# Two weight pieces of even attention split in quarters over four steps each

## The chip, the cores and the metric

The kernel runs on one core of one Trainium2 chip. The time is that of the device in microseconds (us), from the start to the end of one execution. Three executions of the kernel before were timed, and one more was recorded by the hardware profiler. The engines are TensorE (PE, whose weight loads are listed as PEld), VectorE (DVE), ScalarE (ACT), GpSimd (POOL) and SyncE (SP), whose queue issues the loads of weights.

## The reference

Three blocks run one after the other on 512 tokens of width 1024: a layer with even attention, a layer with differential attention, and a third block with neighbourhood attention and a gated recurrence. Each has an MLP of width 4096. The change lies in the first layer, in the attention that follows the input projection:

```python
def even_mixer(h, w_in, cmp_pe, cmp_w1, cmp_w2, w_out, cos, sin):
    ...
    qa = apply_rope(qa.reshape(bsz, T, A_HEADS, HEAD_DIM), cos, sin)
    ...
    o_a = dsa_attention(qa, ka, va, qi, ki, wi)
    ...
    o_b = nsa_attention(qb, k_c, v_c, k_s, v_s, k_w, v_w, gb, cmp_pe, cmp_w1, cmp_w2)
    o = jnp.concatenate([o_a.reshape(bsz, T, -1), o_b.reshape(bsz, T, -1)], axis=-1)
    return jnp.einsum('bte,ed->btd', o, w_out)
```

`dsa_attention` has 8 heads with one shared key and value; each query attends to the 128 keys that an index score picks (top-k). `nsa_attention` has 8 heads in two groups of keys and values and adds three gated branches: compressed, selected and window attention.

## The kernel before

**Weights in pieces and halves.** Products are made in three passes to keep float32 precision: a matrix is split into a high half, rounded to the type fp32r, and a low half, the rest. A product is high times high, high times low, and low times high. Weights come in pieces of 128 partitions by 2048 columns, loaded by SyncE into one of two buffers `stg`. ScalarE makes the high half `wh` (L381), VectorE the low half `wl` = `stg` - `wh` (L385). There are two buffers of each half. `split(e, key, ahead)` (L365) issues engine e's part for all pieces up to one behind `key` in the order in which TensorE takes them (`TAKES`). ScalarE's part waits for the load and for TensorE to have freed the halves of the piece two before; VectorE's waits for ScalarE's. SyncE refills a `stg` buffer when VectorE's part is done.

**The attention loop.** The work is cut into 52 units, each for a pair of heads and (but for the compressed ones) one block of 128 queries. Four groups of nine units come first (`cmp`, then `slc` and `win` for each of four query blocks), then 16 `dsa` units. Each engine runs a loop over steps n, one program per engine, in this order within a step:

- TensorE (`pe_even`): a part of "er" work if there is any, then the products with the values of unit n-4 (L1544, L1550), the transposes of unit n-3 (L1514), the scores of unit n (L1434, L1441, L1438; L1422 and L1425 for `cmp`).
- ScalarE (`act_even`): a rope copy (L1617) in some steps, the high half of a finished pair of heads (L1565) in some, the copy of the transposed weights of unit n-3 (L1530), the exponentials of unit n-1 (L1472), then `split_er`.
- VectorE (`dve_even`): the maximum of unit n-1 (L1461), the low half of a finished pair of heads (L1571) in some steps, the scaling of unit n-2 (L1496 and L1504; L1483 to L1492 for `cmp`), a rope addition (L1629, L1632) in some steps, then `split_er`, then one round of top-k (`take_more`, L1203 and L1205), as long as there are any, up to step 29.

**The "er" work** projects and rotates the queries of later heads in between, in parts of three: x = 0 and x = 1 are twelve matmuls each (L425), x = 2 the rotation (L1595). `ER_AT` puts a part into every third step. Piece `qa0` is taken in step 4, `qa2` in step 22, and the first piece of `out0`, the output projection, from step 50 on. `split_er` runs `split` in the step in which a piece is first taken, so piece `qa2` is split whole in step 4, and piece `("out0", 0, 0)` in step 22, on ScalarE and VectorE in the same step.

All waits are on semaphores, and each engine works through its queue in order. The loop's order is written out by hand.

Of the kernel before, what the change touches and what calls it, by code (L numbers as in the profile page):

```python
# [8 lines left out]
F32 = mybir.dt.float32  # L9
# [3 lines left out]
ALU = mybir.AluOpType  # L13
ACT = mybir.ActivationFunctionType
# [101 lines left out]
def build(nc, ins, out):  # L116
    ctx = ExitStack()
    with ctx:
# [5 lines left out]
        def signal(name, by=1):  # L124
            s = Signal(ctx.enter_context(nc.semaphore(name)), by)
            every.append(s)
            return s
# [86 lines left out]
        p_mm, p_turn, p_rot = signal("p_mm"), signal("p_turn"), signal("p_rot")  # L214
        p_score, p_flip, p_out, p_cmp, p_hg = [signal(n) for n in ("p_score", "p_flip", "p_out", "p_cmp", "p_hg")]
        a_hi, a_sq, a_part, a_keep, a_rope = [signal(n) for n in ("a_hi", "a_sq", "a_part", "a_keep", "a_rope")]
        a_up, a_exp, a_flip, a_misc, a_hg = [signal(n) for n in ("a_up", "a_exp", "a_flip", "a_misc", "a_hg")]
        v_lo, v_add, v_part, v_keep, v_rope = [signal(n) for n in ("v_lo", "v_add", "v_part", "v_keep", "v_rope")]
# [51 lines left out]
        for c in range(2):  # L270
            src = ins["even_w_out"][:, c * 512:(c + 1) * 512]
            piece(("out0", c, 1), 4, 512, [(whole, src[0:512, :].rearrange("(k p) n -> p k n", p=128))])
            hi = src[512:1024, :].rearrange("(g j d) n -> g d j n", g=2, j=4)
# [43 lines left out]
        ORDER, TAKES, SPLITS = [], [], []  # L317
# [4 lines left out]
        def stage_no(key):  # L322

            if is_block(key) and key[3:] == (1, 1):
                return 2
            return [k for k in ORDER if not (is_block(k) and k[3:] == (1, 1))].index(key) % 2

        def stage_of(key):
            kts, ncols, _, _ = SPEC[key]
            return (STG + [third])[stage_no(key)][:, 0:kts * ncols]  # L330

        def halves_of(key):
            kts, ncols, _, _ = SPEC[key]
            b = SPLITS.index(key) % 2
            return WH[b][:, 0:kts * ncols], WL[b][:, 0:kts * ncols]
# [18 lines left out]
        at_split = {}  # L354

        def whole_of(key):

            if key[3:4] != ("P",):
                return stage_of(key), piece_in[stage_no(key)].at(key)
            c = SEVEN[key[4]][1]  # L360
            if c in ("t1", "t2", "t3", "t4"):
                return (SB if c in ("t2", "t4") else SA), v_sum.at(key[0:3] + (c,))
            return stage_of(key[0:3] + c), piece_in[stage_no(key[0:3] + c)].at(key[0:3] + c)

        def split(e, key, ahead=1):  # L365

            last = TAKES.index(key) + ahead
            while at_split[e] <= min(last, len(TAKES) - 1):
                k = TAKES[at_split[e]]
                at_split[e] += 1  # L370
                if SPEC[k][3]:
                    continue
                n = SPLITS.index(k)
                hi, lo = halves_of(k)
                source, ready = whole_of(k)
                if e == "act":
                    act = engine[e]
                    act.wait_ge(*ready)
                    if n >= 2:
                        act.wait_ge(*p_mm.at(("free", SPLITS[n - 2])))  # L380
                    act.activation(hi, source, ACT.Copy).then_inc(*a_hi.next(k))  # L381
                else:
                    dve = engine[e]
                    dve.wait_ge(*a_hi.at(k))
                    dve.tensor_tensor(lo, source, hi.bitcast(F32), ALU.subtract).then_inc(*v_lo.next(k))  # L385

        engine = {}

# [139 lines left out]
        def act_add(act, tag, nk):  # L528
            for c in range(2):
                for g in range(nk // 4):  # L530
                    split("act", tag + (c, g))
                    yield

        def dve_add(dve, tag, nk, banks=range(8)):
            for c in range(2):
                for g in range(nk // 4):
                    split("dve", tag + (c, g))
                    for i in range(NT if g == nk // 4 - 1 else 0):
                        hc = h[:, i, c * 512:(c + 1) * 512]
                        dve.wait_ge(*p_mm.at((tag, c, i)))  # L540
                        dve.tensor_tensor(hc, hc, bank[banks[c * 4 + i]], ALU.add).then_inc(*v_add.next((tag, c, i)))
                    yield
# [56 lines left out]
        def act_add_norm(act, tag, norm, scratch=None):  # L599
# [13 lines left out]
            for g in range(2):  # L613
                split("act", tag + (0, g))
# [717 lines left out]
        def take_more(n):  # L1332
            for _ in range(n):
                next(taking["k"], None)
# [109 lines left out]
        def dve_max(dve, n):  # L1444
            m = small[n % 16]
            dve.wait_ge(*p_score.at(("even", n)))
            if UNITS[n][0] == "cmp":
                v = pair(n).rearrange("p g (a n) -> p g a n", n=32)
                dve.tensor_reduce(m[:, 0:8].rearrange("p (g a) -> p g a", g=2), v, AX.X, ALU.max).then_inc(
                    *v_max.next(("even", n, "max")))  # L1450
                dve.wait_ge(*v_max.now())
                dve.tensor_scalar(m[:, 0:8], m[:, 0:8], -1e28, None, ALU.max).then_inc(*v_max.next(("even", n, "low")))
                dve.wait_ge(*v_max.now())
                if n >= 4:
                    dve.wait_ge(*p_flip.at(("even", n - 4)))
                for g in range(2):
                    t = dve.tensor_tensor(PX[n % 4][:, g, 0:128].rearrange("p (a n) -> p a n", n=32), v[:, g],
                                          m[:, g * 4:g * 4 + 4].unsqueeze(2).to_broadcast([128, 4, 32]), ALU.subtract)
                t.then_inc(*v_max.next(("even", n)))
                return  # L1460
            dve.tensor_reduce(m[:, 0:2], pair(n), AX.X, ALU.max, negate=True).then_inc(*v_max.next(("even", n)))  # L1461
# [105 lines left out]
        def dve_head(dve, n):  # L1567
            if head_end(n):
                tag, j, (hi, lo) = head_end(n)
                dve.wait_ge(*a_part.at((tag, j)))  # L1570
                dve.tensor_tensor(lo, bank[6], hi.bitcast(F32), ALU.subtract).then_inc(*v_part.next((tag, j)))  # L1571

        ER = [(f"qb{j}", ("in", "qb2"), j - 2, qbT[:, j, :]) for j in (2, 3)]
        ER += [(f"qa{j}", ("in", f"qa{j // 2 * 2}"), j % 2, qaT[:, j, :]) for j in range(4)]
        ER_AT = {}
# [48 lines left out]
        def dve_er(dve, m):  # L1625
            name, _, _, dest = ER[m]
            dve.wait_ge(*p_rot.at(name))
            dve.wait_ge(*v_rope.at(ER[m - 2][0] if m >= 2 else f"qb{m}"))
            dve.tensor_tensor(TT[(2 * m + 1) % 4][:, 0:T], er_turned(m), sinT, ALU.mult).then_inc(*v_rope.next((name, "sin")))  # L1629
            dve.wait_ge(*g_cos.at(name))  # L1630
            dve.wait_ge(*v_rope.now())
            dve.tensor_tensor(dest, TT[2 * m % 4][:, 0:T], TT[(2 * m + 1) % 4][:, 0:T], ALU.add).then_inc(*v_rope.next(name))  # L1632

        def split_er(name, n):
            if n in ER_AT and ER_AT[n][1] == 0 and ER[ER_AT[n][0]][2] == 0:
                split(name, ER[ER_AT[n][0]][1])

        def pe_even(pe):

# [15 lines left out]
        def act_even(act):  # L1655
            for n in range(N_UNITS + 4):
                if n in ER_COPY:
                    act_er(act, ER_COPY[n])
                if n >= 4:
                    act_head(act, n - 4)  # L1660
                if 0 <= n - 3 < N_UNITS:
                    act_flip(act, n - 3)
                if 0 <= n - 1 < N_UNITS:
                    act_exp(act, n - 1)
                split_er("act", n)
                yield

        def dve_even(dve):
            for n in range(N_UNITS + 5):
                if 0 <= n - 1 < N_UNITS:  # L1670
                    dve_max(dve, n - 1)
                if n >= 5:
                    dve_head(dve, n - 5)
                if 0 <= n - 2 < N_UNITS:
                    dve_prob(dve, n - 2)
                if n in ER_AT and ER_AT[n][1] == 2:
                    dve_er(dve, ER_AT[n][0])
                split_er("dve", n)
                take_more(1)
                yield  # L1680

# [1701 lines left out]
```

## Time and profile before

| | us |
|---|---|
| median of 3 runs | 2228.25 |
| lowest and highest | 2227.51, 2230.23 |
| profiled execution, its own time | 2233.16 |
| span of the profiled execution | 2231.4 |
| TensorE busy in the span | 2131.4 |
| VectorE busy in the span | 1355.6 |
| ScalarE busy in the span | 920.9 |

### The profile page before, as it was taken

How to read it: one execution, taken by the hardware profiler on the slowest of the kernel's cores; microseconds unless marked ns; L12 is line 12 of the kernel's file. 1: busy time of each engine (PE TensorE's matmuls, PEld its weight loads, DVE VectorE, ACT ScalarE, POOL GpSimd, SP SyncE). 2: the span in 40 equal slices, each digit the busy share in tenths (PEclk: the TensorE clock that was granted, in tenths of full speed). 3: DMA queues.
4: the chain of work that ended last, by engine and by line, in shares of the span. 5: the costliest groups of instructions: out<-in, count | busy, mean ns of one | idle time of the engine just before them, and what ended most of it. 6: DMA issues, size and time to landing. Idle time of an engine off the chain costs nothing.

```text
span 2231.4 us, 27080 instructions
## 1 busy us (share of the span) xinstructions
PE 2131.4 (96%) x10767; PEld 1682.5 (75%) x10771; DVE 1355.6 (61%) x1995; ACT 920.9 (41%) x1485; POOL 223.3 (10%) x212
## 2 busy tenths in 40 slices
PE   6878888999999999999999999999999999999998
PEld 5765556888888776678888888766778768888887
DVE  4568853687773446756877745355656424678753
ACT  3214553545443334445454443143423223544542
POOL 2210000000000011100000003011145421000000
PEclk9989989999999999999999999999999999999999
DMA  5430101223332221113333323221112213342232
GB/s 143 116 95 20 20 1 57 95 95 113 105 100 98 79 76 57 38 57 104 95 114 111 97 95 108 79 63 47 57 50 65 72 42 114 104 132 82 97 105 76
DMA packets 163511, 182.64 MB, mean 82 GB/s; under 512 B 19701, under 2 KB 123562, under 8 KB 163386
## 3 DMA queue, kind: packets, MB, share of 16 engines
q1 hardware_dynamic: 161066, 174.11, 24.9%
q0 software_dynamic: 2320, 6.80, 1.2%
q8 instruction: 86, 1.41, 0.3%
q14 instruction: 39, 0.32, 0.0%
HBM read 177.75 MB, written 2.17 MB: 81 GB/s over the span
## 4 chain that ended last, share of the span: by engine, by line
PE 86%; DVE 8%; ACT 3%; issue 2%; DMA 1%; SPq 1%; POOL 0%; ACTq 0%; POOLq 0%; DVEq 0%
PE banks L425 70%; PE banks L2761 2%; DVE wl L385 2%; ACT wh L381 2%; PE banks L1514 1%; PE banks L1434 1%; PE banks L1550 1%; PE banks L2880 1%; DVE uTl L595 1%; PE banks L1958 1%; PE banks L2020 1%; PE banks L2451 1%; PE banks L2530 1%; PE banks L1882 1%; PE banks L2501 1%
## 5 line engine op out<-in xcount | busy, mean ns | idle before, releaser
L425 PE MATMUL banks<-uTh,wh 128*128 128x512 f32 (+1 forms) x1408 | 554.6, 394 | 14.1 <-DVE wl L385 4.2
L425 PE MATMUL banks<-uTl,wh 128*128 128x512 f32 (+1 forms) x1408 | 539.1, 383 | 0.0
L425 PE MATMUL banks<-uTh,wl 128*128 128x512 f32 (+1 forms) x1408 | 539.0, 383 | 0.0
L425 PE MATMUL banks<-wh,hTr 128*128 128x512 f32 x1552 | 487.4, 391 | 0.3 <-DVE hTr L2080 0.3
L385 DVE TENSOR_TENSOR wl<-stg,wh 128x2048 fp32r<-128x2048 f32 (+1 forms) x136 | 313.7, 2307 | 244.8 <-ACT wh L381 244.2
L381 ACT ACTIVATE wh<-stg 128x2048 fp32r<-128x2048 f32 (+1 forms) x136 | 258.6, 1902 | 209.2 <-PE banks L425 175.0
L425 PEld LDWEIGHTS banks<-wh,hTr 128*128 128x128 f32 x1552 | 291.6, 188 | 64.4 <-DVE wl L385 2.5
L425 PEld LDWEIGHTS banks<-uTh,wh 128*128 128x128 f32 x1408 | 268.6, 191 | 70.6 <-issue 10.3
L425 PEld LDWEIGHTS banks<-uTh,wl 128*128 128x128 f32 x1408 | 267.7, 190 | 52.4
L425 PEld LDWEIGHTS banks<-uTl,wh 128*128 128x128 f32 x1408 | 268.6, 191 | 50.2 <-issue 2.4
L425 PE MATMUL banks<-wl,hTr 128*128 128x512 f32 x776 | 302.5, 390 | 0.0
L425 PEld LDWEIGHTS banks<-wl,hTr 128*128 128x128 f32 x776 | 145.9, 188 | 29.2
L805 ACT ACTIVATE p<-banks 128x512 f32<-128x512 f32 x96 | 57.4, 597 | 209.1 <-PE banks L425 209.1
L502 POOL TENSOR_TENSOR nrm<-nrm,half 128x1 f32<-128x1 f32 x28 | 15.4, 551 | 1210.8 <-DVE nrm L649 1188.5
L425 PE MATMUL banks<-wh,uTh 128*128 128x512 f32 (+1 forms) x256 | 100.7, 393 | 10.9 <-DVE wl L385 6.3
L823 DVE TENSOR_TENSOR hTr<-p,hTr 128x512 fp32r<-128x512 f32 (+1 forms) x132 | 78.8, 614 | 33.5 <-ACT hTr L818 33.3
L425 PE MATMUL banks<-wh,uTl 128*128 128x512 f32 (+1 forms) x256 | 98.6, 385 | 0.0
L425 PE MATMUL banks<-wl,uTh 128*128 128x512 f32 (+1 forms) x256 | 98.5, 385 | 0.0
L838 DVE TENSOR_TENSOR p<-p 128x256 f32<-128x256 f32 x36 | 15.2, 423 | 107.4 <-ACT p L807 107.4
L818 ACT ACTIVATE hTr<-p 128x512 fp32r<-128x512 f32 (+1 forms) x132 | 71.9, 564 | 19.7 <-DVE p L840 18.1
L1530 ACT ACTIVATE big<-banks 128x256 f32<-128x256 f32 (+3 forms) x52 | 35.3, 679 | 83.7 <-PE banks L1514 83.7
L909 DVE TENSOR_TENSOR h<-h,big 128x512 f32<-128x512 f32 x108 | 68.8, 686 | 0.3
(381 smaller groups left out, 2798.1 us busy)
## 6 DMA issues: line engine op xcount, KB each, us to landing
stg<-mlp_w_up SPq DMA_DIRECT2D x32, 1024.0 KB, 5.3
stg<-mlp_w_down SPq DMA_DIRECT2D x26, 1024.0 KB, 5.2
stg<-w_in SPq DMA_DIRECT2D x20, 1024.0 KB, 5.2
stg<-w_up SPq DMA_DIRECT2D x16, 1024.0 KB, 5.3
stg<-w_down SPq DMA_DIRECT2D x13, 1024.0 KB, 5.2
stg<-odd_w_in SPq DMA_DIRECT2D x16, 512.0 KB, 4.6
big<-mlp_w_down SPq DMA_DIRECT2D x6, 1024.0 KB, 7.6
stg<-even_cmp_w SPq DMA_DIRECT2D x4, 1024.0 KB, 5.4
```

The lines of the kernel that those rows point to most:

```text
L381: act.activation(hi, source, ACT.Copy).then_inc(*a_hi.next(k))
L385: dve.tensor_tensor(lo, source, hi.bitcast(F32), ALU.subtract).then_inc(*v_lo.next(k))
L425: t = pe.matmul(outp, x, y, start=(start and k == 0 and m == 0), stop=(stop and k == n - 1 and m == 2))
L595: dve.scalar_tensor_tensor(out=uTl[:, k, s], in0=norm_rows(norm, ph, k), scalar=col(gname, g0 + k), in1=uTh[:, k, s].bitcast(F32), op0=ALU ...
L805: act.activation(r, up_bank(tag, j), ACT.Relu).then_inc(*a_up.next((tag, "relu", q, j)))
L818: act.activation(hi, v, ACT.Copy).then_inc(*a_up.next((tag, n, what)))
L823: dve.tensor_tensor(lo, v, hi.bitcast(F32), ALU.subtract).then_inc(*v_up.next((tag, n, what)))
L909: x = dve.tensor_tensor(hc, hc, v, ALU.add)
L1434: pe.matmul(b[:, g, :], qv[p, j, i * 128:(i + 1) * 128], kv[p, 0:w], start=True, stop=False)
L1514: t = pe.transpose(b[:, g, s], p[:, g, s], ident)
L1530: act.activation(dest, turned(n), ACT.Copy).then_inc(*a_flip.next(("even", n)))
L2761: t = pe.matmul(b, fill_w["y"][:, k, f * 128:(f + 1) * 128], (onT, ohT)[br][:, k, :], start=(k == 0), stop=(k == 3))
```

## The change

The two pieces are no longer split by `split` in steps 4 and 22. A new function `split_part` makes a quarter, 512 of the 2048 columns. ScalarE's quarters of `qa2` stand in steps 8 to 11 and those of `("out0", 0, 0)` in steps 24 to 27; VectorE's stand one step behind, in steps 9 to 12 and 25 to 28, at the same place within a step as before. ScalarE's first quarter carries the two waits of the whole piece, and each quarter of VectorE waits for ScalarE's quarter. The signal that the piece is ready, for which TensorE and SyncE wait, comes with VectorE's last quarter.

```diff
+        def split_part(e, key, x, parts):
+
+            assert TAKES[at_split[e]] == key
+            n = SPLITS.index(key)
+            hi, lo = halves_of(key)
+            source, ready = whole_of(key)
+            s = slice(x * 2048 // parts, (x + 1) * 2048 // parts)
+            last = x == parts - 1
+            if e == "act":
+                act = engine[e]
+                if x == 0:
+                    act.wait_ge(*ready)
+                    act.wait_ge(*p_mm.at(("free", SPLITS[n - 2])))
+                act.activation(hi[:, s], source[:, s], ACT.Copy).then_inc(*a_hi.next((key, x), *([key] if last else [])))
+            else:
+                dve = engine[e]
+                dve.wait_ge(*a_hi.at((key, x)))
+                dve.tensor_tensor(lo[:, s], source[:, s], hi[:, s].bitcast(F32), ALU.subtract).then_inc(
+                    *v_lo.next((key, x), *([key] if last else [])))
+            if last:
+                at_split[e] += 1
+
...
+        ER_SPLITS = {8: ("in", "qa2"), 24: ("out0", 0, 0)}
+
         def split_er(name, n):
-            if n in ER_AT and ER_AT[n][1] == 0 and ER[ER_AT[n][0]][2] == 0:
-                split(name, ER[ER_AT[n][0]][1])
+            for n0, key in ER_SPLITS.items():
+                if n0 <= n < n0 + 4:
+                    split_part(name, key, n - n0, 4)
...
-                split_er("dve", n)
+                split_er("dve", n - 1)
```

## Rows read from the trace of the kernel before

**Rows 1.** The page's busy times: engine, us busy, share of the span, instructions.

```profile
PE 2131.4 (96%) x10767; PEld 1682.5 (75%) x10771; DVE 1355.6 (61%) x1995; ACT 920.9 (41%) x1485; POOL 223.3 (10%) x212
```

**Rows 2.** Stretches of 20 us: busy us of each engine, TensorE's clock, DMA share, GB/s.

```profile
160.00:180.00 20.00, 12.02 (x59) 7.65 (x58) 13.57 (x36) 6.43 (x21) 0.00 (x0) 0.76 0.09 28
```

**Rows 3.** Timeline, steps 4 to 8: start, us, engine, line, operation, idle before.

```profile
171.87 0.28 PE L1441 MATMUL banks<-causal,identb 128*128 128x128 bf16 x2
...
172.52 1.92 ACT L381 ACTIVATE wh<-stg 128x2048 fp32r<-128x2048 f32 x1
...
173.89 0.28 PE L1441 MATMUL banks<-causal,identb 128*128 128x128 bf16 x2
...
174.47 2.29 DVE L385 TENSOR_TENSOR wl<-stg,wh 128x2048 fp32r<-128x2048 f32 x1 [5.90 <-ACT wh L381]
...
174.76 0.44 PE L1550 MATMUL banks<-big 128*64 128x128 f32 x4 [0.58 <-ACT big L1530]
...
177.81 0.68 DVE L1461 TENSOR_REDUCE sm<-banks 128x2 f32<-128x512 f32 x1
...
179.39 1.12 PE L1514 MATMUL banks<-k_c_ident,big 128*128 128x128 f32 x4 [4.18 <-DVE big L1504]
...
188.80 1.23 DVE L1461 TENSOR_REDUCE sm<-banks 128x2 f32<-128x1024 f32 x1 [2.55 <-PE banks L1441]
```

**Rows 4.** Timeline, steps 22 to 26, VectorE and TensorE.

```profile
239.30 2.29 DVE L385 TENSOR_TENSOR wl<-stg,wh 128x2048 fp32r<-128x2048 f32 x1 [2.45 <-ACT wh L381]
...
244.22 1.11 PE L1514 MATMUL banks<-k_c_ident,big 128*128 128x128 f32 x4 [4.18 <-DVE big L1504]
...
253.66 1.22 DVE L1461 TENSOR_REDUCE sm<-banks 128x2 f32<-128x1024 f32 x1 [2.58 <-PE banks L1441]
```

**Rows 5.** Timeline, steps 15 and 17, VectorE and TensorE.

```profile
210.52 0.66 PE L1514 MATMUL banks<-k_c_ident,big 128*128 128x128 f32 x4
...
217.75 1.23 DVE L1461 TENSOR_REDUCE sm<-banks 128x2 f32<-128x1024 f32 x1 [0.35 <-PE banks L1441]
```

**Rows 6.** Stretches before and after the first stall, columns as in rows 2.

```profile
171.00:174.00 3.00, 3.00 (x25) 1.51 (x23) 0.00 (x0) 2.66 (x6) 0.00 (x0) 1.00 0.00 0
...
179.40:184.00 4.60, 4.60 (x14) 2.84 (x15) 4.50 (x11) 1.97 (x7) 0.00 (x0) 0.50 0.43 161
```

**Rows 7.** Timeline of VectorE, step 10: the rope addition and the next instruction.

```profile
199.05 0.69 DVE L1632 TENSOR_TENSOR big<-t 128x512 f32<-128x512 f32 x1
...
199.66 0.56 DVE L1203 MAX8 m<-big 128x8 f32<-128x384 f32 x1
```

**Rows 8.** Timeline of VectorE and TensorE, steps 14, 29 and 30.

```profile
209.73 0.73 DVE L1504 TENSOR_SCALAR big<-big,sm,gate 128x256 f32<-128x256 f32 x2
...
267.07 0.50 DVE L1492 TENSOR_TENSOR big<-big,sm 128x128 f32<-128x128 f32 x2
...
267.72 0.44 PE L1514 MATMUL banks<-k_c_ident,big 128*128 128x128 f32 x2
```

**Rows 9.** Timeline of ScalarE, steps 9 and 12.

```profile
193.30 0.81 ACT L1530 ACTIVATE big<-banks 128x768 f32<-128x768 f32 x1 [0.96 <-PE banks L1514]
...
202.98 0.60 ACT L1565 ACTIVATE qr<-banks 128x512 fp32r<-128x512 f32 x1 [0.50 <-PE banks L1550]
```

**Rows 10.** Timeline of TensorE behind two equal pauses.

```profile
300.00 0.47 PE L1550 MATMUL banks<-big 128*64 128x128 f32 x4 [2.01 <-DVE hTr L1571]
...
309.99 1.09 PE L1550 MATMUL banks<-big 128*64 128x128 f32 x16
...
315.06 0.44 PE L1550 MATMUL banks<-big 128*64 128x128 f32 x4 [2.01 <-DVE uTl L1571]
...
322.24 1.09 PE L1550 MATMUL banks<-big 128*64 128x128 f32 x16
```

**Rows 11.** Timeline of SyncE's queue: the loads behind the two splits.

```profile
176.79 0.39 SPq L418 DMA_DIRECT2D stg<-even_w_out  x1
...
241.62 1.61 SPq L418 DMA_DIRECT2D stg<-even_w_out  x2
```

## The prediction

> **What bounds the kernel now.** I read the page's busy times first: TensorE is busy for 96% of the span [rows 1], so most of the kernel moves only with TensorE, and a split can matter only where TensorE stands still. Next the table of 20 us stretches, to find such places in even attention: in 160 to 180 us TensorE is busy 12.02 of 20 us, at a mean granted clock of 0.76 [rows 2]. Then the timeline around the two split pieces, and last the list of waits, to see who is released by whom.
>
> Step 4 of the attention loop holds the split of piece qa2 [rows 3]. ScalarE converts the whole piece from 172.52 (1.92 us). VectorE has had nothing to do for 5.90 us when it starts its part at 174.47 (2.29 us), because its split stands in the same step and is queued ahead of its own maximum of unit 4. That maximum reads scores that TensorE finished at 171.87 + 0.28 = 172.15, yet it starts at 177.81. Behind it are queued the scaling of unit 3 and so TensorE's transposes of unit 3, which start at 179.39 after 4.18 us of idle. The stall is a loop: VectorE waits for ScalarE, TensorE for VectorE. Step 22 repeats it for the first piece of out0: VectorE idle 2.45 us, its part 2.29 us, TensorE idle 4.18 us again [rows 4].
>
> The pause costs a second time. After it the granted clock is 0.50, the 1.2 GHz level, with TensorE busy throughout [rows 6]. From the transposes that end the stall to VectorE's maximum in step 8 (26) it takes 188.80 - 179.39 = 9.41 us [rows 3] and 253.66 - 244.22 = 9.44 us [rows 4]; the same instructions, same widths, one pair of heads later at full clock (steps 15 to 17) take 217.75 - 210.52 = 7.23 us [rows 5]. In both places VectorE ends by waiting for TensorE (2.55 and 2.58 us), so TensorE sets the pace there and the slow clock is paid: 2.18 and 2.21 us.
>
> **The change, part by part.** *Removed from step 4.* TensorE's next work without the split is: scores of unit 5, done at 173.89 + 0.28 = 174.17; products of unit 2, 0.44 us long, of which I let 0.33 pass before the next start; then the transposes of unit 3 at 174.50. VectorE is ready for them: its maximum can start at 172.2, 5.6 us earlier than 177.81, and it has the scaling of unit 3 done before 174. So the transposes move from 179.39 to 174.50: 4.89 us. TensorE then has no pause before them, which I take to mean that the clock stays up: 2.18 us more. Sum at the maximum of step 8: 7.07 us.
>
> *Removed from step 22.* Here VectorE sets the start. It was free at 239.30 - 2.45 = 236.85 and goes on behind the split at 239.30 + 2.29 - 0.08 = 241.51, the 0.08 being how far instructions overlap [rows 7]; without the split it goes on at about 236.85 - 0.08. I take 4.74 us. With the clock, 2.21: 6.95 us at the maximum of step 26.
>
> *Added: eight quarters on VectorE.* No row has this instruction at 512 columns. The nearest is the rope addition, 128x512 f32 from SBUF into SBUF: 0.69 us long, but the next instruction starts 0.61 us after it [rows 7]. I take 0.61 as the time one quarter holds the queue. The bounds: 2.29 / 4 = 0.57 if nothing is paid for each instruction, 0.69 if nothing overlaps. Four cost 2.44 (2.3 to 2.8) us.
>
> How many are exposed? For qa2 they stand in VectorE's steps 9 to 12. Step 15's transposes start 0.05 us after VectorE's scaling ends (209.73 + 0.74 = 210.47, against 210.52) [rows 5, 8], so by then everything that VectorE is late, TensorE is late too. All four are exposed: 2.44 us. For out0 they stand in steps 25 to 28. Quarter one falls into the idle of 2.58 us, of which 2.58 - 2.21 = 0.37 is left once the clock is up; 0.24 is exposed. The other three are exposed in front of step 30's transposes of the compressed unit, with 267.72 - (267.07 + 0.50) = 0.15 us, less the 0.06 that a release takes, of slack [rows 8]. So 0.24 + 1.83 - 0.09 = 1.98 us. After step 29 the top-k rounds are used up and VectorE has slack.
>
> A rule of the Trainium skill speaks against quarters. Rows 7 and the whole piece give 0.69 and 2.29 us: four times 512 columns are 0.47 us longer than once 2048. "VectorE: DVE Perf Modes", section on the TRN2 errata, says that each instruction with SBUF sources pays a fixed latency, a large tile once and small tiles every time, and recommends tiles of at least 512 elements. The trace agrees in the durations; the start of the next instruction gives 0.08 of it back. By the rule without that overlap, the 7.4 exposed quarters would cost 0.6 us more, and the gain would be 9.0 instead of 9.6 us.
>
> *Added: eight quarters on ScalarE*, 0.60 us each as its 512-column copy into fp32r [rows 9], about 0.5 of it in the queue. Each stands behind the exponentials and ahead of the next copy of transposed weights, before which ScalarE idles for 0.96 us (step 9) and for 0.50 us even in the tight step 12 [rows 9]; the 1.92 us of the whole piece goes. I count nothing. If the cover were gone, TensorE would get its copies up to 0.5 us late each time, 3.9 us in all. Each quarter is done a step before VectorE asks for it, so its wait holds up nothing.
>
> *Moved: two loads.* SyncE's queue waits for VectorE's last part before it refills the buffer. It issues two loads of out0 at 176.79 and about 241.6 [rows 11]; they move to about 200 and 254. Their pieces are split only after the attention loop, which still runs at 322 us [rows 10]: hidden by more than 60 us. The two moved pieces are used in steps 22 and 50; they are ready in steps 12 and 28.
>
> **Sum.** qa2: 7.07 - 2.44 = 4.63. out0: 6.95 - 1.98 = 4.97. Together 9.6 us. Behind the loop TensorE is the bound and takes the shift through to the end. The profiled execution would go from 2233.16 (span 2231.4 and 1.8 around it) to 2223.6. It lies 4.9 us over the median of the runs, 2228.25; the median would become 2218.6. Faster or slower by 0.2% is 4.5 us, about what a measurement of this kernel can tell from no change.
>
> **The rivals.** *A new pause lowers the clock.* Where VectorE is late before step 30's transposes, TensorE now stands for about 1.9 us. A pause of 2.01 us before 300.00 was followed by low clock, an equal one before 315.06 was not. The same instructions then took 309.99 - 300.00 = 9.99 us against 322.24 - 315.06 = 7.18 us [rows 10]: a fall costs 2.8 us. Gain 6.8, time 2221.4. Chance 0.22.
>
> *The later pauses fall out otherwise.* The shift changes which of the pauses near 300, 315 and 327 us are followed by low clock: one fewer gives 2215.8, one more 2221.4. "TensorE: Matmul & The Clock Gate", section on the HAM clock gate, says the activity monitor runs free of the kernel's start; whether the same pause is followed by a fall may then differ from run to run, which fits the pair above. Chance 0.12 for one fewer; one more is inside the rival before.
>
> *The stalls go, but the clock is low all the same*, because of the earlier fall at step 2 or of VectorE's pace. Then 4.4 us of the sum is missing: gain about 5.3, time 2223. Against it: the granted clock is 1.00 in 171 to 174 us with TensorE busy all of the 3.00 us [rows 6], and nothing in the argument above leaves it idle there. Chance 0.07.
>
> *The change does nothing*: each stall is only handed on, because VectorE must do the 2.29 us anyway and was the bound. Then the gain is at most the wait for ScalarE. It speaks against this that VectorE idles 2.55 and 2.58 us afterwards, waiting for TensorE. Time 2225 to 2228. Chance 0.05.
>
> *Slower*: the four steps in which VectorE is now late make TensorE pause in each, and the clock falls again and again there. At 2.8 us for a fall, the fourth makes the kernel slower than now, and five give 14 - 9.6 = 4.4 us slower, 2232.7. For it: pauses as short as 2.01 us did it once. Against it: the present pauses of 0.5 us in that stretch, at full clock, grow by no more than about 1 us each. Chance 0.03.
>
> **How the numbers follow.** The forecast, 2218.6, has a chance of 0.51; its own range with 0.57 to 0.69 us for a quarter and a little ScalarE delay is 2217.5 to 2220. The range of 2214.5 to 2223.3 takes in the clock rivals on both sides. Faster by over 0.2% (below 2223.8): the forecast, both first rivals, most of the third, 0.89. Same 0.08, slower 0.03.
>
> **What would show it.** Right: no TensorE idle over 1 us in steps 5 to 8 or 23 to 26; granted clock 1.00 from about 171 us to beyond 250; VectorE's quarters near 0.69 us long with no idle before them; the maximum of step 8 near 181.7 instead of 188.8; step 15's transposes 4.6 us earlier than 210.52; step 30's 9.6 us earlier than 267.72, after an idle of nearly 2 us. Wrong: transposes that wait for ScalarE's copies; a low clock in 190 to 215 us; quarters longer than 0.7 us; or a stretch behind the attention loop that gives the shift back.

## The result, and the profile after

The changed kernel takes 2219.06 us in the median of 6 runs (2218.55 to 2223.38), the kernel before 2227.88 us in 6 runs (2224.81 to 2230.23). The ratio is 0.9963, with a 95% interval of 0.9951 to 0.9975: 8.2 us, or 0.4%, faster. The forecast was 2218.6 us and a gain of 9.6 us. Repeated in two later groups, the ratio was 0.9950 (0.9937 to 0.9963) and 0.9963 (0.9949 to 0.9977).

The timeline of the changed kernel, VectorE and TensorE in steps 4 to 8. Lines behind the inserted function are 22 higher than before: L1483 is the maximum, L1526 the scaling, L1536 the transposes, L404 a quarter of the low half:

```profile
172.60 0.69 DVE L1483 TENSOR_REDUCE sm<-banks 128x2 f32<-128x512 f32 x1 [2.51 <-PE banks L1463]
...
174.89 0.66 PE L1536 MATMUL banks<-k_c_ident,big 128*128 128x128 f32 x4
...
182.13 1.22 DVE L1483 TENSOR_REDUCE sm<-banks 128x2 f32<-128x1024 f32 x1 [1.06 <-PE banks L1463]
```

The maximum of unit 4 still waits, but for its own scores. The transposes of unit 3 follow with no idle time in front of them, and take 0.66 us where they took 1.12 [rows 3]. This execution entered the loop 0.4 us later than the one before (165.68 against 165.27 for the first maximum of step 2). With 0.40 us taken off, the transposes are 4.90 us earlier than in [rows 3] and the maximum of step 8 is 7.07 us earlier; the prediction had 4.89 and 7.07. The clock in these stretches, columns as in [rows 2], answers to [rows 2, 6]:

```profile
160.00:180.00 20.00, 16.79 (x94) 10.85 (x92) 16.85 (x49) 6.83 (x25) 0.00 (x0) 0.83 0.01 1
...
175.00:182.00 7.00, 7.00 (x44) 4.32 (x44) 5.92 (x15) 2.98 (x9) 0.00 (x0) 1.00 0.01 2
...
240.00:249.00 9.00, 9.00 (x83) 5.53 (x78) 8.86 (x17) 6.15 (x14) 1.27 (x1) 1.00 0.01 3
```

TensorE is busy 16.79 us instead of 12.02 in the stretch from 160 to 180, at a mean clock of 0.83 instead of 0.76 [rows 2]. The low clock that the changed kernel has in this stretch lies before 171 us, where the kernel before has it too. From 175 to 182 us the clock is 1.00; behind the stall of the kernel before it was 0.50 [rows 6].

The quarters of qa2 on VectorE, with the instruction behind the first of them, and TensorE's idle time in steps 12 to 15:

```profile
188.56 0.69 DVE L404 TENSOR_TENSOR wl<-stg,wh 128x512 fp32r<-128x512 f32 x1
...
189.16 0.42 DVE L1225 MAX8 m<-big 128x8 f32<-128x256 f32 x1
...
197.29 0.44 PE L1536 MATMUL banks<-k_c_ident,big 128*128 128x128 f32 x2 [1.03 <-DVE big L1514]
...
203.08 0.44 PE L1566 MATMUL banks<-big 128*64 128x128 f32 x4 [0.62 <-DVE qr L1593]
...
206.26 0.66 PE L1536 MATMUL banks<-k_c_ident,big 128*128 128x128 f32 x4 [0.70 <-DVE big L1526]
...
213.49 1.23 DVE L1483 TENSOR_REDUCE sm<-banks 128x2 f32<-128x1024 f32 x1 [0.36 <-PE banks L1463]
```

No quarter has idle time in front of it. The first lasts 0.69 us and holds the queue for 0.60 us. TensorE now waits 1.03, 0.62 and 0.70 us for VectorE, together 2.35 us. It is 2.41 us late at step 15: 7.07 us earlier at step 8, 4.66 at step 15.

Steps 25 to 30, with GpSimd's rope product beside VectorE's scaling, answer to [rows 4, 8]:

```profile
240.88 0.69 DVE L404 TENSOR_TENSOR wl<-stg,wh 128x512 fp32r<-128x512 f32 x1
...
242.61 1.22 DVE L1483 TENSOR_REDUCE sm<-banks 128x2 f32<-128x1024 f32 x1
...
243.94 1.92 DVE L1526 TENSOR_SCALAR big<-big,sm,gate 128x384 f32<-128x384 f32 x2
...
243.97 1.27 POOL L1645 TENSOR_TENSOR t<-p,k_c_cos 128x512 f32<-128x512 f32 x1 [28.21 <-ACT p L1639]
...
250.15 1.09 PE L1536 MATMUL banks<-k_c_ident,big 128*128 128x128 f32 x8 [0.25 <-DVE big L1526]
...
258.19 0.49 DVE L1514 TENSOR_TENSOR big<-big,sm 128x128 f32<-128x128 f32 x2
...
258.74 0.44 PE L1536 MATMUL banks<-k_c_ident,big 128*128 128x128 f32 x2 [1.66 <-DVE big L1514]
```

The quarter of step 25 stands where VectorE was idle for 2.58 us, most of it because TensorE was slow; the maximum of step 26 now starts without idle time. The transposes of step 30 follow 1.66 us of idle and start 9.38 us earlier than before, once the 0.4 us are taken off; the prediction had 9.6, and nearly 2 us for the idle time. SyncE's loads of out0 moved as described, to 200.91 us and later, and nothing waits for them.

To compare kernels whose loops begin at different times, I use the distances between five marks (points that every version has): TensorE's transposes of unit 0 (164.02 before), VectorE's maximum in step 8, its maximum in step 17, TensorE's transposes in step 30, and the first matmul of the MLP (363.06 before). Each is a difference of two starts in the timelines, in us. The last column is the profiled execution's own time; one execution is not the median.

| version | to step 8 | to 17 | to 30 | to the MLP | own time |
|---|---|---|---|---|---|
| before | 24.78 | 28.95 | 49.97 | 95.34 | 2233.16 |
| changed | 17.71 | 31.36 | 45.25 | 92.37 | 2218.88 |
| changed, second group | 16.19 | 31.33 | 45.20 | 93.67 | 2215.80 |
| changed, third group | 17.19 | 31.37 | 45.23 | 95.30 | 2221.06 |
| only qa2 | 17.66 | 31.34 | 50.52 | 93.81 | 2225.55 |
| only out0 | 24.12 | 28.94 | 45.21 | 95.37 | 2225.18 |
| whole, one step apart | 17.17 | 31.17 | 43.97 | 95.33 | 2222.32 |
| quarters, same step | 17.68 | 34.37 | 48.35 | 93.71 | 2229.23 |
| before, TensorE kept busy | 21.09 | 28.96 | 47.74 | 92.38 | 2219.99 |
| VectorE's quarters twice | 16.33 | 36.20 | 47.03 | 95.25 | 2231.42 |
| ScalarE's quarters twice | 16.28 | 31.35 | 45.28 | 97.05 | 2220.06 |
| before, ScalarE a step ahead | 16.62 | 28.96 | 45.20 | 92.33 | 2212.85 |
| quarters in idle time | 17.67 | 28.97 | 42.99 | 93.68 | 2211.59 |
| whole in idle time | 17.73 | 28.94 | 42.99 | 96.60 | 2215.26 |

The columns up to step 30 repeat within 0.1 us where the code is the same, except where the clock differs: a low stretch that began before step 4 ends sooner or later, which moves the first column by 1.5 us. The column to the MLP moves by 5 us (92.3 to 97.1), for code that is the same in all but the last two rows. It goes with the low clock: behind step 30 and up to the pause in front of the MLP, TensorE spends 6.8 us at the low level in the versions with 92.3 to 92.4, 10.2 us in those with 93.7 to 93.8, 13.7 us in those with 95.2 to 95.4, and 17.1 us in the one with 97.05. The one version off this line is "whole in idle time" (13.7 us at the low level and 96.60), which is taken up below. The executions of the kernel before scatter from 2222.3 to 2235.3 us over all groups, with mean granted clocks between 0.987 and 0.981 in the third group. So the medians answer questions of 3 us and more, the marks those of tenths.

### The profile page after: what moved, and what is told of

Same layout as the page of the kernel before. It is cut to its first block, busy times and chain, and to the rows that moved or that the text cites. A ratio compares the mean times of both kernels' runs of the same rounds, so it can differ in the third digit from the quotient of the medians.

```text
span 2217.1 us, 27096 instructions
## 1 busy us (share of the span) xinstructions
PE 2122.2 (96%) x10771; PEld 1676.2 (76%) x10771; DVE 1360.1 (61%) x2001; ACT 921.9 (42%) x1491; POOL 221.3 (10%) x212
## 4 chain that ended last, share of the span: by engine, by line
PE 85%; DVE 9%; ACT 2%; issue 2%; DMA 1%; SPq 1%; POOL 0%; POOLq 0%; ACTq 0%; DVEq 0%
PE banks L447 70%; PE banks L2787 2%; DVE wl L385 2%; ACT wh L381 2%; PE banks L2906 1%; PE banks L1536 1%; PE banks L1456 1%; DVE uTl L617 1%; PE banks L1572 1%; DVE big L1227 1%; DVE sm L1483 1%; PE banks L2046 1%; DVE big L1526 1%; PE banks L1984 1%; PE banks L2477 1%
## 5 line engine op out<-in xcount | busy, mean ns | idle before, releaser
L447 PE MATMUL banks<-wh,uTh 128*128 128x512 f32 (+1 forms) x256 | 100.5, 392 | 10.9 <-DVE wl L385 6.3
L659 DVE TENSOR_TENSOR h<-h,banks 128x512 f32<-128x512 f32 x48 | 32.9, 685 | 58.6 <-PE banks L447 58.6
```

Source lines behind the costliest of these rows:

```text
L447: t = pe.matmul(outp, x, y, start=(start and k == 0 and m == 0), stop=(stop and k == n - 1 and m == 2))
```

## The experiments

Ratios are to the kernel before, timed in the same group. The changed kernel itself was timed again in the second and in the third group. Four experiments (TensorE kept busy, quarters in the same step, VectorE's quarters twice, quarters in idle time) were timed in another group without it, so a comparison of their medians with the changed kernel's goes across groups.

**The change once more**, as the reference of the second group and, with the expectation "9 to 11 us less", of the third.

> The changed kernel once more, as the common reference of this group. My account (two loops of waits taken out, quarters partly exposed on VectorE) expects 8.5 to 9.6 us less than the kernel before.

> The changed kernel once more as reference of this group: 9 to 11 us less than the kernel before.

Medians 2218.03 and 2219.35 us, ratios as given above: 11.1 us less, more than the first expectation, and 8.2 us less, less than the second (10.0 by the medians). In the third group's profile the clock fell behind the idle time of step 30, in the two others it didn't:

```profile
258.42 0.44 PE L1536 MATMUL banks<-k_c_ident,big 128*128 128x128 f32 x2 [1.66 <-DVE big L1514]
```

```profile
258.90:262.00 3.10, 3.10 (x11) 2.06 (x12) 3.03 (x11) 1.19 (x5) 0.00 (x0) 0.50 0.98 188
```

Pauses are equal (1.66 us here and in the first profile), the clock is 0.50 after this one. The rival of a new pause that lowers the clock is real, in some executions. From this pause to VectorE's next long wait, in step 35, it is 16.30 us here and 14.72 and 14.69 in the two others, so this fall cost 1.6 us.

**One piece at a time.**

```diff
         def split_er(name, n):
-            for n0, key in ER_SPLITS.items():
-                if n0 <= n < n0 + 4:
-                    split_part(name, key, n - n0, 4)
+            for key, x, parts in PARTS[name].get(n, ()):
+                split_part(name, key, x, parts)
...
-                split_er("dve", n - 1)
+                split_er("dve", n)
```

`PARTS` lists for each engine and step the piece, the part and the number of parts. For qa2 alone it has qa2's quarters as in the change and, for both engines, `22: [(("out0", 0, 0), 0, 1)]`: the whole piece in step 22. For out0 alone it has out0's quarters and `4: [(("in", "qa2"), 0, 1)]`.

> Only piece qa2 in quarters (steps 8 to 11 and 9 to 12); the first piece of out0 whole in step 22 on both engines, as before. My account: 4.6 us less than before (7.07 for the stall and its slow clock, less 2.44 for four exposed quarters), and the stall of about 4.2 us with low clock behind it still there in step 24. Rival, that one of the two stalls was merely handed on: 0 or the whole 9 us.

> Only the first piece of out0 in quarters (steps 24 to 27 and 25 to 28); qa2 whole in step 4, as before. My account: 4.8 to 5.0 us less than before. With the run of qa2 alone the two gains should add up to that of the whole change. Rival: the gains overlap, and the sum is over 2 us off.

qa2 alone: median 2224.55 us, ratio 0.9978 (0.9967 to 0.9989), 4.9 us. out0 alone: 2223.28 us, 0.9972 (0.9962 to 0.9982), 6.2 us. The sum, 11.1 us, is that of the whole change in the same group, though each of the two is known only to about 2.3 us. The stalls stand where they were left, in the first kernel in step 24, in the second in step 6:

```profile
239.83 1.11 PE L1536 MATMUL banks<-k_c_ident,big 128*128 128x128 f32 x4 [4.18 <-DVE big L1526]
```

```profile
177.81 1.12 PE L1536 MATMUL banks<-k_c_ident,big 128*128 128x128 f32 x4 [4.18 <-DVE big L1526]
...
262.20 0.44 PE L1536 MATMUL banks<-k_c_ident,big 128*128 128x128 f32 x2 [1.65 <-DVE big L1514]
```

```profile
262.00:266.00 4.00, 3.80 (x14) 2.55 (x15) 3.93 (x13) 1.19 (x5) 0.00 (x0) 0.61 1.01 197
```

The gains add up; no stall is handed on. By the marks, out0 alone gains 4.76 us in the third column, and qa2 alone 7.12 in the first less 2.39 in the second. In the second kernel the clock falls behind the new pause of step 30 as well.

**What the low clock costs.** The kernel before, with TensorE kept busy in its two stalls:

```diff
         def pe_flip(pe, n):
             b, p = turned(n), PX[n % 4]
+            if n in (3, 21):
+                pe.wait_ge(*a_flip.at(("even", n - 1)))
+                for _ in range(24):
+                    pe.transpose(b[:, 0, 0:128], ident, ident)
             pe.wait_ge(*v_prob.at(("even", n)))
```

> The kernel before, with 24 transposes of the identity matrix on TensorE (results unused) while it waits in steps 6 and 24, before the wait for VectorE's scaling. The stalls of 4.2 us stay, TensorE is only kept busy in them. If the slow clock after them costs 2.2 us each, as I took it: clock 1.00 in 179 to 184 and 244 to 249 us, and 4.4 us less than before. If the clock costs nothing, because VectorE would have been the bound: no difference.

Median 2223.01 us, ratio 0.9976 (0.9965 to 0.9986): 5.4 us less for 48 useless transposes. The transposes of unit 3 in step 6, and the maximum of step 8:

```profile
178.93 0.66 PE L1518 MATMUL banks<-k_c_ident,big 128*128 128x128 f32 x4 [1.41 <-DVE big L1504]
...
186.16 1.23 DVE L1461 TENSOR_REDUCE sm<-banks 128x2 f32<-128x1024 f32 x1 [0.35 <-PE banks L1441]
```

They last 0.66 us instead of 1.12, and it is 7.23 us to the maximum, the value of [rows 5], instead of 9.41. From step 17 to 30 the kernel takes 47.74 us against 49.97: 2.23 us for the second stall. The stalls themselves are as long as before. So of the 7 us that such a stall cost up to the next mark, 2.2 came after it. It is not the same in every execution: from the transposes behind the stall to the maximum it is 10.01 us with qa2 alone and 10.24 us with out0 alone, 2.8 and 3.0 us more than 7.23. There the clock fell 0.7 and 0.3 us before the stall ended, in [rows 3, 4] 2.0 us before, so more of a low stretch of the same length lay behind it.

**The distance or the size?** Whole pieces with VectorE one step behind:

```diff
+        PARTS = {"act": {8: [(("in", "qa2"), 0, 1)], 24: [(("out0", 0, 0), 0, 1)]},
+                 "dve": {9: [(("in", "qa2"), 0, 1)], 25: [(("out0", 0, 0), 0, 1)]}}
```

And the change's quarters, with VectorE's in the same step as ScalarE's:

```diff
-                split_er("dve", n - 1)
+                split_er("dve", n)
```

> No quarters: each piece whole, ScalarE in step 8 (24) and VectorE one step behind in 9 (25). Theory A, the distance between the two engines' parts takes the stall away, and the quarters do nothing: the time of the changed kernel or 0.4 us less, because four instructions of 0.61 us become one of 2.21 us. Theory B, the small size matters, because a whole piece holds up the maximum and the scaling behind it, and TensorE pauses over 2 us: slower than the changed kernel by 2 to 5 us, with a low clock in 190 to 200 or 245 to 255 us.

> Quarters in steps 8 to 11 and 24 to 27 on both engines: VectorE's quarter in the same step as ScalarE's. If the distance of one step matters, VectorE waits about 1.2 us for each quarter of ScalarE, behind its exponentials; with nearly all of it exposed, the time is 5 to 8 us over that of the changed kernel. If the quarters alone did the work: equal to the changed kernel.

Whole: median 2220.82 us, ratio 0.9959 (0.9947 to 0.9971), against 0.9950 (0.9937 to 0.9963) for the changed kernel of the group; the intervals overlap. Up to step 30 it is at least as fast: 31.17 against 31.33, and 43.97 against 45.20 us. Its clock never falls between steps 5 and 30. Theory A holds there; that its median is 2.8 us higher isn't explained by anything up to step 30, and whether the later stretches would repeat it is open.

Quarters in the same step: median 2225.49 us, ratio 0.9996 (0.9985 to 1.0007). In the median the gain is gone; by the marks, 3.3 of the 9.4 us up to step 30 are left (100.40 us against 103.70 before and 94.32 changed). VectorE waits for ScalarE in front of a quarter, in the lines of steps 8 and 9:

```profile
186.27 0.69 DVE L404 TENSOR_TENSOR wl<-stg,wh 128x512 fp32r<-128x512 f32 x1 [1.21 <-ACT wh L400]
...
191.52 0.69 DVE L404 TENSOR_TENSOR wl<-stg,wh 128x512 fp32r<-128x512 f32 x1 [0.92 <-ACT wh L400]
```

Up to step 17 it loses 3.0 us: two waits for ScalarE, 2.13 us together, and 0.66 us more of waiting for TensorE at step 17 (1.02 against 0.36), whose clock had fallen at about 202 us. Up to step 30 it loses another 3.1 us; the four waits there (0.97, 0.84, 1.05, 0.93 us) are 3.79 us, so not all of it was exposed. The clock fell again at about 253 us. Measured by the marks it is 6.1 us over the changed kernel, within the 5 to 8 that were expected. The stalls of 4.18 us are gone here too, in their place stand TensorE pauses of up to 1.67 us. So quarters without the distance of a step keep a third of the gain up to step 30, and the distance without quarters keeps all of it.

**What the quarters cost.** Each twice on VectorE, and, as a kernel of its own, each twice on ScalarE, the first time into `spare` (128x512, bf16):

```diff
+                dve.wait_ge(*v_lo.now())
+                dve.tensor_tensor(spare, source[:, s], hi[:, s].bitcast(F32), ALU.subtract).then_inc(*v_lo.next())
                 dve.tensor_tensor(lo[:, s], source[:, s], hi[:, s].bitcast(F32), ALU.subtract).then_inc(
...
+                act.wait_ge(*a_hi.now())
+                act.activation(spare, source[:, s], ACT.Copy).then_inc(*a_hi.next())
                 act.activation(hi[:, s], source[:, s], ACT.Copy).then_inc(*a_hi.next((key, x), *([key] if last else [])))
```

> The changed kernel with each of VectorE's eight quarters done twice (the first time into a spare buffer in bf16). By my count of exposed quarters the added eight at 0.61 us cost 4.4 to 4.9 us over the changed kernel. If VectorE has slack in these steps, less than 1 us.

> The changed kernel with each of ScalarE's eight quarters done twice (the first time into a spare buffer in bf16). I counted ScalarE's quarters at nothing, hidden in its idle time: within 1 us of the changed kernel. If they were exposed, about 0.5 us for each of the eight: 4 us slower.

VectorE twice: median 2227.04 us, 8 us over the changed kernel's 2219.2, more than expected. Three rows show why:

```profile
198.98 0.44 PE L1539 MATMUL banks<-k_c_ident,big 128*128 128x128 f32 x2 [2.24 <-DVE big L1517]
...
205.96 0.44 PE L1569 MATMUL banks<-big 128*64 128x128 f32 x4 [1.81 <-DVE qr L1596]
...
218.81 1.23 DVE L1486 TENSOR_REDUCE sm<-banks 128x2 f32<-128x1024 f32 x1 [2.79 <-PE banks L1466]
```

TensorE's pause in step 12 is now 2.24 us, and the clock stays at 1.00 for over 8 us behind it. It falls behind the next pause, of 1.81 us before 205.96 (low from 207.6 to 214.3 us), and at step 17 VectorE waits 2.79 us for TensorE instead of 0.36. Of the 4.84 us by which the second column grows, 2.43 are this wait; the other 2.41 are four more quarters at 0.60 us. This is the price that was assumed, and a fall of the clock comes on top of it. Which pause brings one can't be told by its length: 2.24 us didn't, 1.81 us did.

ScalarE twice: median 2219.72 against 2219.35 us, and 31.35 and 45.28 us between the marks, as in the changed kernel. ScalarE's quarters cost nothing in these stretches, even doubled. (The 97.05 us of its column to the MLP go with a fall of the clock behind step 30.)

**Where there is idle time.** From the trace of the changed kernel I took the places where VectorE is idle: 2.51 us in step 4, and 1 to 2 us in front of most maxima from step 38 on.

In quarters, ScalarE splits qa2 in steps 0 to 3 and VectorE all of it in step 4; out0 follows in steps 38 to 41 and 39 to 42. Whole, the edit to the `PARTS` of above is:

```diff
-        PARTS = {"act": {8: [(("in", "qa2"), 0, 1)], 24: [(("out0", 0, 0), 0, 1)]},
-                 "dve": {9: [(("in", "qa2"), 0, 1)], 25: [(("out0", 0, 0), 0, 1)]}}
+        PARTS = {"act": {3: [(("in", "qa2"), 0, 1)], 38: [(("out0", 0, 0), 0, 1)]},
+                 "dve": {4: [(("in", "qa2"), 0, 1)], 39: [(("out0", 0, 0), 0, 1)]}}
```

> Quarters where VectorE is idle: qa2 on ScalarE in steps 0 to 3, all four of VectorE's in step 4, where the trace of the changed kernel shows it idle for 2.51 us before the maximum of unit 4; out0 in steps 38 to 41 (39 to 42), where it idles about 2 us in each step and there is no top-k. By my account the 2.4 and 2.0 us that the quarters cost go away: 3 to 4.4 us less than the changed kernel. If a quarter on ScalarE is exposed in the second place (its exponentials are waited for there), 1 to 2 us of it are lost.

> Whole pieces in the places where VectorE is idle: qa2 on ScalarE in step 3 and VectorE in step 4, out0 in steps 38 and 39. If only place and distance count, the time of the version with quarters in the same places (about 4 us less than the changed kernel). If a whole piece of 1.9 and 2.3 us is too large for the second place, where ScalarE and VectorE are waited for in every step: 1 to 2 us more than that.

Quarters: median 2214.72 us, ratio 0.9945 (0.9929 to 0.9961). Whole: 2217.90 us, ratio 0.9949 (0.9933 to 0.9966). The four quarters stand in front of the top-k round of step 4, and the maximum of step 8 is where it was in the changed kernel:

```profile
168.86 2.49 DVE L404 TENSOR_TENSOR wl<-stg,wh 128x512 fp32r<-128x512 f32 x4
...
182.07 1.23 DVE L1483 TENSOR_REDUCE sm<-banks 128x2 f32<-128x1024 f32 x1 [1.07 <-PE banks L1463]
...
211.04 1.23 DVE L1483 TENSOR_REDUCE sm<-banks 128x2 f32<-128x1024 f32 x1 [0.35 <-PE banks L1463]
```

The second and third columns are 28.97 and 42.99 us: the gain of 6.98 us in the third is the 6.95 that the prediction had for the second stall with nothing exposed, and the second column is that of the kernel before. Up to step 30 this version is 4.7 us faster than the changed kernel. Its median, the lowest of the study, is 4.5 us below the 2219.2 of the 23 runs of the changed kernel; but the intervals of the ratios overlap, and the five runs are few.

With whole pieces the marks up to step 30 are the same, so in step 4 the size makes no difference. In steps 38 and 39 it does:

```profile
283.53 2.29 DVE L404 TENSOR_TENSOR wl<-stg,wh 128x2048 fp32r<-128x2048 f32 x1 [0.81 <-ACT wh L400]
...
287.70 0.69 PE L1572 MATMUL banks<-big 128*64 128x128 f32 x4 [3.71 <-DVE hTr L1593]
```

VectorE waits 0.81 us for ScalarE's whole piece, one step apart, and TensorE's pause is 3.71 us; with quarters it is 2.01, as in the kernel before. From step 30 to the end of this pause it is 33.96 us against 32.26 with quarters: 1.7 us, within the 1 to 2 that the expectation gave for a piece that is too large for this place. The medians lie 3.2 us apart the same way, across groups.

**The least edit.** The kernel before, ScalarE one step ahead:

```diff
-                split_er("act", n)
+                split_er("act", n + 1)
```

> The kernel before with one thing moved: ScalarE splits one step earlier (steps 3 and 21), whole; VectorE stays whole in steps 4 and 22. If the wait for ScalarE is the core of the stall and VectorE's own 2.3 us cost only where it has no idle time: in step 4 they fit into an idle time of 2.5 us and cost nothing (7.1 us gained up to the maximum of step 8, nothing lost in steps 9 to 15); in step 22 they stay exposed, TensorE waits about 1.7 us instead of 4.2, and 2.45 us are gained, 4.6 if the clock stays up. In all 9.5 to 11.7 us less than before, so at least as good as the changed kernel without any quarter. If the small size is what counts: worse than the changed kernel by 3 us or more.

Median 2221.68 us, ratio 0.9961 (0.9945 to 0.9976), close to the changed kernel's 0.9963. It gained 8.7 us, less than the 9.5 to 11.7 expected. In the second and third columns together it was 2.45 us faster (74.16 us against 76.61). What is left of the two stalls:

```profile
174.01 0.66 PE L1514 MATMUL banks<-k_c_ident,big 128*128 128x128 f32 x4 [0.36 <-DVE big L1504]
...
234.15 0.66 PE L1514 MATMUL banks<-k_c_ident,big 128*128 128x128 f32 x4 [2.32 <-DVE big L1504]
```

0.36 us where VectorE's 2.3 us fit into idle time, 2.32 where they don't (expected: 1.7). Nothing but the distance of a step was changed here, so the wait for ScalarE made 3.8 of the 4.2 us of the first stall and 1.9 of the second; the rest of the second is VectorE's own part. In this execution the clock didn't fall behind the 2.32 us. The runs scatter from 2212.85 to 2224.81 us, so the median doesn't bear out what the marks promise. The profiled execution is the fastest of the eleven, with a mean granted clock of 0.989 against 0.984 to 0.987 in the others. So the others had more low clock; where in the kernel, no trace shows.

## Why the prediction was right

**Time.** 2219.06 us against 2218.6, gain 8.8 us by the medians and 8.2 by the ratio against 9.6. The mechanism was the one described, at the places described; the later groups, at 8 to 11 us, leave it there. That the medians agree to 0.5 us is luck: those of the changed kernel alone lie between 2218.0 and 2219.4 in the three groups, and the interval of the ratio allows gains from 5.6 to 10.9 us. The firm number is the gain up to step 30 in the profiles, 9.38 us against 9.6.

**The removed stalls.** 7.07 us up to step 8 was exact for the two executions compared, in which the low clock before step 4 ended at the same place. In the second and third groups it ended earlier or began earlier, and the first column gives 8.59 and 7.59. The runs with one piece each show the two independent.

**The clock.** Taking 2.2 us for each stall from a stretch of the same instructions at full clock was right: 2.18 and 2.23 us with TensorE kept busy in the stalls. The two stalls in the runs with one piece cost 2.8 and 3.0 us in this way.

**The quarters.** Assumed 0.61 us each, seen 0.60. Four exposed for qa2: 31.36 - 28.95 = 2.41 us against 2.44. For out0 the term was 1.98 us, and the estimate of it from the traces is 45.25 - 42.99 = 2.26 us, the version in idle time having none. The 0.28 us come from a stall that the prediction had not seen, 0.37 us, less 0.1 us in the other terms (the first quarter exposed by 0.19 instead of 0.24, and 0.60 instead of 0.61 for the others). VectorE's scaling in step 26 takes 0.87 us if GpSimd is idle, 1.55 in the kernel before, where GpSimd's rope product begins 0.32 us ahead of it, and 1.92 here, where the product begins 0.03 us after it. With the whole piece one step apart VectorE is later still, GpSimd is done, and the scaling takes its 0.87 us:

```profile
242.88 1.27 POOL L1645 TENSOR_TENSOR t<-p,k_c_cos 128x512 f32<-128x512 f32 x1 [27.71 <-ACT p L1639]
...
244.92 0.87 DVE L1526 TENSOR_SCALAR big<-big,sm,gate 128x384 f32<-128x384 f32 x2
```

These 1.05 us are most of the 1.3 us by which that version's third column is below the changed kernel's. With ScalarE's quarters twice the product begins later, in the midst of the scaling, and the quarter behind it is held up instead, by as much (1.76 us instead of 0.69); the product takes 1.44 us instead of 1.27:

```profile
244.16 1.44 POOL L1648 TENSOR_TENSOR t<-p,k_c_cos 128x512 f32<-128x512 f32 x1 [28.73 <-ACT p L1642]
...
244.39 1.76 DVE L407 TENSOR_TENSOR wl<-stg,wh 128x512 fp32r<-128x512 f32 x1
```

The Trainium skill has the rule: "SBUF — State Buffer", section "SBUF: two separate sides", says that a GpSimd instruction and a VectorE instruction in a mode with two ports, or with two SBUF inputs against a GpSimd instruction that reads SBUF, share one pair of ports, which the one that starts first holds to its end while the other waits. These rows agree that the two hold each other up; they don't show which ports.

**The rule on small tiles.** With its 0.69 us and no overlap the cost would have been 0.6 us higher; the start-to-start distance of 0.60 us decided against it. In place, four quarters cost 2.41 us and the whole piece 31.17 - 28.95 = 2.22: small tiles cost 0.19 us here, not the 0.47 of the durations.

**ScalarE at nothing, the loads at nothing.** The doubled run and the unchanged marks confirm the one (a quarter is 0.61 to 0.64 us long, 0.60 was taken). For the other, the loads were issued at 200.91 us and later, and nothing waited.

**The rivals.** A new pause that lowers the clock (0.22): in one of the three profiles of the changed kernel, and in those of out0 alone and of ScalarE twice. Its chance was too low as a thing that happens, and its price too high: 1.6 us in the changed kernel's profile and with out0 alone (16.24 us to step 35 against 14.7), 2.8 only with ScalarE twice (17.52), where the low stretch is twice as long. How many of the timed executions had such a fall isn't known. The later pauses (0.12 for one fall fewer): they did fall out otherwise. Of the three pauses of 2.01 us, the first and the third were followed by low clock in the kernel before, 6.8 us each, the second and the third in the changed kernel, 3.4 us each, and all three in its second and third profiles, 3.4 us each. Slower, by a clock that falls again and again: it took twice the quarters, or quarters in the same step, to bring one fall into steps 9 to 16. The change doing nothing, and a clock that stays low: neither was seen. (Two slips in the working change nothing: 0.74 us is read where [rows 8] has 0.73, and 9.6 less 4.4 is 5.2, not 5.3.)

**What the median doesn't show of the sum.** The profiled execution gained 14.3 us, of which 9.4 up to step 30. The other 4.9 lie in stretches of unchanged code, 2.97 of them before the MLP, where the two low stretches of the clock behind 300 us were half as long as before (6.8 us at the low level in all against 13.7). The second and third profiles had 10.2 and 13.7 us between step 30 and the MLP. This is the scatter of the clock and no gain of the change.

## What to carry to other kernels

When two engines share a job one after the other, and each has other work in an ordered queue, put the second part at least one step behind the first: that took away 4 us stalls here, in quarters or whole, while quarters in the same step kept a third of the gain up to step 30 and none in the median. Then ask where the second engine is idle and put its part there; the same work cost 2.4 us where it was exposed and nothing five steps earlier. The size counts where the piece is longer than the gap: in steps 38 and 39 a whole piece cost 1.7 us and the quarters nothing. Count a TensorE stall with the stretch of low clock behind it, priced from the same instructions at full clock.

## What the runs showed of the hardware that was not expected

The same pause doesn't always have the same sequel. After 1.66 us of idle in step 30 the granted clock stayed at 1.00 in one execution and fell to 0.50 in another. Low stretches at the same place of the loop differ in length too: behind the last of the three pauses of 2.01 us, before 327.31 in the kernel before and before 316.88 in the changed one, the clock was low for 6.8 and for 3.4 us. Here are the two stretches of the changed kernel, and one of the kernel before that is twice as long, behind the pause before 300.00; behind the same pause (before 291.02) the changed kernel's clock stayed at 1.00. The columns are those of [rows 2]. Over a whole execution this makes a scatter of 13 us for one kernel (2222.3 to 2235.3), more than the change is worth.

```profile
304.60:307.60 3.00, 3.00 (x20) 2.21 (x18) 1.47 (x4) 1.74 (x5) 0.00 (x0) 0.51 0.00 0
...
318.00:320.90 2.90, 2.90 (x19) 2.15 (x20) 1.36 (x4) 1.89 (x5) 0.00 (x0) 0.50 0.00 0
```

```profile
300.40:307.00 6.60, 6.60 (x35) 4.13 (x36) 1.96 (x6) 3.44 (x10) 0.00 (x0) 0.50 0.01 2
```

GpSimd's product of 1.27 us lengthens VectorE's pair of scalings from 0.87 us to 1.30, 1.55 or 1.92 us, where it begins 0.57 or 0.32 us before the scaling or 0.03 us after its start. In all three cases the scaling ends 0.60 to 0.62 us after the product. A product that begins 0.55 us after the scaling's start leaves it at 0.87 us and holds up the next VectorE instruction.
